# Expert results scaled by their gates and added in DRAM by the scatter itself, with the last norm in the experts' Block

## What is computed

```python
h2 = rmsnorm_2(x, norm2_w)
p_group = softmax(h2 @ wg + bg);  pg, g_sel = top_k(p_group, 1)
top_v, top_i = top_k(expert logits within group g_sel, 2)
gates = softmax(top_v) * pg                      # two gates per token
for each pair (token, expert):                   # 1024 x 2 = 2048 pairs
    y = (silu(h2 @ w_gate[e]) * (h2 @ w_up[e])) @ w_down[e]
    x[token] += gate * y
out = rmsnorm_2(x, norm_f_w)
```

## Time and profile before

| | |
|---|---|
| median of 3 runs | 3539.9 us (3534.38 to 3540.42) |
| profiled execution | 3536.11 us, of which the span from first to last instruction 3534.4 us |
| mean granted TensorE clock | 0.958 |
| experts, from the first gather's issue to the last scatter's | 2882.5 to 3483.1 us |
| last two Blocks, from the last scatter's issue to the end | 3483.05 to 3534.4 us |

### The profile page before, as it was taken

How to read it: one execution, slowest core, us unless ns; L and a number is a source line. 1 busy time by engine, 2 the same in 40 slices (tenths; PEclk the granted TensorE clock), 3 DMA queues, 4 the chain that set the end, 5 groups by cost and what they waited for, 6 DMA issues and landing times. The chain is left out here.

```text
span 3534.4 us, 38476 instructions
## 1 busy us (share of the span) xinstructions
PE 3233.8 (91%) x14690; PEld 2651.4 (75%) x14690; DVE 1920.6 (54%) x2268; ACT 1309.2 (37%) x1660; POOL 326.7 (9%) x356
## 2 busy tenths in 40 slices
PE   6999999899999999999799999969958849999993
PEld 5888888787878888888687778857647738788882
DVE  4344443434345455445511755439636469889985
ACT  4233222312321111111521233325334338888883
POOL 0000000000000000000010000034123101111100
PEclk9999999999999999999899999979979969999996
DMA  3222222242221111111232233342054149999995
GB/s 103 67 67 66 78 84 85 99 157 79 77 84 36 54 53 36 53 54 42 78 117 59 84 106 122 107 164 108 27 181 147 51 159 387 371 372 379 384 363 210
DMA packets 324127, 472.48 MB, mean 134 GB/s; under 512 B 62864, under 2 KB 227216, under 8 KB 321968
## 3 DMA queue, kind: packets, MB, share of 16 engines
q1 hardware_dynamic: 294528, 384.31, 31.9%
q0 software_dynamic: 29488, 86.67, 6.6%
HBM read 414.14 MB, written 73.53 MB: 138 GB/s over the span
## 5 line engine op out<-in xcount | busy, mean ns | idle before, releaser
L1106 DVE TENSOR_TENSOR x_rows<-x_rows,ff_psd 128x512 f32<-128x512 f32 x336 | 228.7, 687 | 304.0 <-PE ff_psd L378 303.9
L376 PE MATMUL m_ps<-h_hl,m_w_hl 128*128 128x512 f32 x896 | 356.4, 398 | 6.7 <-PEq L315 6.7
L377 PE MATMUL m_ps<-h_hl,m_w_hl 128*128 128x512 f32 x896 | 349.9, 391 | 0.0
L378 PE MATMUL m_ps<-h_hl,m_w_hl 128*128 128x512 f32 x896 | 349.9, 390 | 0.0
L2770 DVE TENSOR_TENSOR h_hl<-ex_stage,h_hl 128x1024 fp32r<-128x1024 f32 x256 | 307.3, 1221 | 45.4 <-ACT h_hl L2766 43.9
L2766 ACT ACTIVATE h_hl<-ex_stage 128x1024 fp32r<-128x1024 f32 x256 | 270.7, 1060 | 85.0 <-DMA ex_stage<-in_exp_w_up_dram 39.4
L376 PE MATMUL n_turned<-h_hl,pc_w_hl 128*128 128x512 f32 x576 | 225.8, 392 | 6.6 <-DVE pc_w_hl L1479 6.6
L377 PE MATMUL n_turned<-h_hl,pc_w_hl 128*128 128x512 f32 x576 | 224.9, 390 | 0.0
L378 PE MATMUL n_turned<-h_hl,pc_w_hl 128*128 128x512 f32 x576 | 224.7, 390 | 0.0
L376 PEld LDWEIGHTS m_ps<-h_hl,m_w_hl 128*128 128x128 f32 x896 | 168.9, 189 | 45.5 <-DVE m_w_hl L353 7.1
L1081 ACT ACTIVATE ff_act_hl<-ff_act 128x1024 fp32r<-128x1024 f32 x22 | 23.3, 1060 | 473.9 <-DVE ff_act L1130 473.9
(11 more groups left out here) (524 smaller groups left out, 7562.9 us busy)
## 6 DMA issues: line engine op xcount, KB each, us to landing
ex_stage<-in_exp_w_gate_dram SPq DMA_DIRECT2D x128, 512.0 KB, 5.7
ex_stage<-in_exp_w_up_dram SPq DMA_DIRECT2D x128, 512.0 KB, 6.5
ex_stage<-in_exp_w_down_dram SPq DMA_DIRECT2D x128, 512.0 KB, 6.3
m_stage<-in_w_in_dram SPq DMA_DIRECT2D x56, 512.0 KB, 4.5
pc_stage<-in_w_in_dram SPq DMA_DIRECT2D x36, 512.0 KB, 3.8
ff_stage<-in_w_ffn_down_dram SPq DMA_DIRECT2D x22, 512.0 KB, 3.6
ff_stage<-in_w_ffn_gate_dram SPq DMA_DIRECT2D x21, 512.0 KB, 4.7
ff_stage<-in_w_ffn_up_dram SPq DMA_DIRECT2D x21, 512.0 KB, 5.9
```

What stands on the lines that cost most here:

```text
L376: nc.tensor.matmul(out, w_hl[0], x_hl[0], start=first, stop=False)
L377: nc.tensor.matmul(out, w_hl[0], x_hl[1], start=False, stop=False)
L378: return nc.tensor.matmul(out, w_hl[1], x_hl[0], start=False, stop=last)
L1106: v.tensor_tensor(dst, dst, ps_d[g % NB][:], ALU.add).then_inc(s_add, 1)
```

## The change

The gate moves from the last stage into the experts, the sum of the two experts' rows moves from DVE into the scatter, and the two last Blocks go.

- `mlstm_chunks` also stores each finished tile of x to a DRAM tensor `scr.sum` (`sums_out`, on SP).
- Gates by place: POOL writes `in_tile` anew, now with the gate in place of the pair's number (`place_gates`, 16 instructions), PE forms the 16 products with `in_slot` after expert 0's gate product, ACT copies the result to `scr.place_gate`. `in_slot` lies in `ys`, not in `xg`, so it survives until then, and the gather of expert 1 no longer waits for the routing's end.
- `rows_out` multiplies by the place's gate while it copies.
- `store` scatters by token row (`scr.lst`) into `scr.sum` with `compute_op=ALU.add`: the DMA adds to what stands there. An expert holds a token at most once, and each scatter waits until the one before it has landed.
- Further tiles run in the experts' Block, with the experts' buffers, behind a branch on each engine.
- The last norm runs there too: SP waits for all scatters, loads 8 tiles of the sum into `x_tm`, ACT and DVE norm them, SP stores them from `x_tm`. The gain is loaded, and the table of Sqrt (`warm`), before that.

The program of the further tiles, here left out, is that of before with other buffers and the scatter as above.

```diff
@@ mlstm_chunks, SP
+            def sums_out(t):
+                sp.wait_ge(d_add, 2 * t + 2)
+                sp.dma_start(scr.sum[t * P:(t + 1) * P, :], x_tm[:, t]).then_inc(s_sum, 16)
+
             for k in range(2, NC):
                 chunk_loads(k)
+                if k >= 4:
+                    sums_out(k - 4)
+            for t in range(NC - 4, NC):
+                sums_out(t)
+            sp.wait_ge(s_sum, 16 * NC)
@@ route
-    in_slot = mem.xg[:].rearrange("p b (j n) -> p (b j) n", n=P)
+    in_slot = mem.ys[:].rearrange("p b (j n) -> p (b j) n", n=P)
+    def place_gates(pool):
+        pool.wait_ge(mem.s_gates, 1)
+        for j in range(2 * T):
+            t, n = divmod(j, 2)
+            nc.gpsimd.tensor_scalar(in_tile[:, t, n], io[:, 0:NT], tl[:, n, t:t + 1], scr.gate[:, n, t:t + 1], ALU.is_equal,
+                                    ALU.mult).then_inc(mem.s_placed, 1)
-            ch.inc(v.tensor_copy(scr.row[:], pair))
@@ experts, SP, behind the loads of the weights
+            sp.dma_start(rowg[:], A.norm_f_w_2.rearrange("(a n) -> a n", a=1).broadcast_to([P, D])).then_inc(s_g, 16)
+            for b in range(2):
+                sp.wait_ge(s_st[b], 16 * (NE // 2))
+            sp.wait_ge(s_all, 1)
+            for t in range(T):
+                sp.dma_start(x_tm[:, t], scr.sum[t * P:(t + 1) * P, :]).then_inc(s_y[t], 16)
+            for t in range(T):
+                sp.wait_ge(s_res, t + 1)
+                sp.dma_start(out[t * P:(t + 1) * P, :], x_tm[:, t]).then_inc(s_out, 16)
+            sp.wait_ge(s_out, 16 * T)
@@ experts, POOL
             def store(e):
                 pool.wait_ge(s_ys, e + 1)
-                pool.indirect_dma_start(out=scr.ys, out_offset=bass.IndirectOffsetOnAxis(ap=scr.row[:, e:e + 1], axis=0),
-                                        in_=ys[:, e % 2], in_offset=None, bounds_check=PAIRS - 1,
+                if e:
+                    pool.wait_ge(s_st[1 - e % 2], 16 * ((e + 1) // 2))
+                pool.indirect_dma_start(out=scr.sum, out_offset=bass.IndirectOffsetOnAxis(ap=scr.lst[:, e:e + 1], axis=0),
+                                        in_=ys[:, e % 2], in_offset=None, bounds_check=ROWS - 1, compute_op=ALU.add,
                                         oob_is_err=False).then_inc(s_st[e % 2], 16)
+            nc.gpsimd.memset(xg[:], 0.0).then_inc(s_zero, 1)
+            nc.gpsimd.memset(eps[:], EPS).then_inc(s_eps, 1)
...
-                if e == 0:
-                    pool.wait_ge(mem.s_routed, 1)
+                if e == 1:
+                    mem.place_gates(pool)
...
-            for b in range(2):
-                pool.wait_ge(s_st[b], 16 * (NE // 2))
+            pool.wait_ge(mem.s_routed, 1)
+            n = pool.value_load(count, min_val=0, max_val=NX)
+            with pool.If(n > 0):
...
+            pool.sem_inc(s_all, 1)
@@ experts, ACT
                         x_high(e + 1, 1 - b)
+                        if first:
+                            act.wait_ge(s_pm, 1)
+                            nc.scalar.activation(scr.place_gate[:], mem.ps_places, ACT.Copy).then_inc(s_pg, 1)
...
-                nc.scalar.activation(ys[:, b], ps_d[:], ACT.Copy).then_inc(s_ys, 1)
+                act.wait_ge(s_pg, 1)
+                gate = scr.place_gate[:, e:e + 1] if isinstance(e, int) else scr.place_gate[:, bass.ds(e, 1)]
+                nc.scalar.activation(ys[:, b], ps_d[:], ACT.Copy, scale=gate).then_inc(s_ys, 1)
...
+            for_tiles(act, further_start, further)
+            act.wait_ge(s_eps, 1)
+            nc.scalar.activation(warm[:], eps[:], ACT.Sqrt)
+            for t in range(T):
+                act.wait_ge(s_y[t], 16)
+                nc.scalar.activation(square, x_tm[:, t], ACT.Square, accum_out=ssq[:, 0, t:t + 1]).then_inc(s_sq, 1)
+                act.wait_ge(s_sq, t + 1)
+                nc.scalar.activation(ssq[:, 1, t:t + 1], ssq[:, 0, t:t + 1], ACT.Sqrt, scale=1.0 / D, bias=eps[:]).then_inc(s_std, 1)
@@ experts, DVE
+            for_tiles(dve, lambda: dve.sem_inc(x_lo, 1), further)
+            dve.wait_ge(s_g, 16)
+            for t in range(T):
+                dve.wait_ge(s_std, t + 1)
+                v.reciprocal(ssq[:, 2, t:t + 1], ssq[:, 1, t:t + 1]).then_inc(s_rs, 1)
+                dve.wait_ge(s_rs, t + 1)
+                v.scalar_tensor_tensor(x_tm[:, t], x_tm[:, t], ssq[:, 2, t:t + 1], rowg[:], ALU.mult, ALU.mult).then_inc(s_res, 1)
@@ experts, PE
+            def place_gates():
+                for j in range(2 * T):
+                    pe.wait_ge(mem.s_placed, j + 1)
+                    last = nc.tensor.matmul(mem.ps_places, mem.in_slot[:, j], mem.in_tile[:, j // 2, j % 2], start=j == 0,
+                                            stop=j == 2 * T - 1)
+                last.then_inc(s_pm, 1)
...
                     hidden(e, b, ps_g, 0)
+                    if isinstance(e, int) and e == 0:
+                        place_gates()
                     if not (last and b == 1):
                         turn(e + 1, 1 - b)
@@ program
-        routed_experts(nc, A, scr, hl)
-        further_tiles(nc, A, scr)
-        combine(nc, A, scr, x_tm, out[0])
+        routed_experts(nc, A, scr, hl, x_tm, out[0])
```

More of the change, by code:

```diff
@@ L2719, in expert_memory, with experts @@
     return mem
-def experts(nc, A, scr, c, block, mem):
+def experts(nc, A, scr, c, block, mem, x_tm, out):
     NE, D, F = A.exp_w_gate_2.shape[1:]
     KT, FT, NU, NS = D // P, F // P, 12, 6
-    PAIRS = 2 * scr.T * P
+    ROWS, T, NX = scr.T * P, scr.T, scr.NX
     assert NE % 2 == 0 and F == 512 and D == 1024
@@ L2737, in experts, with for_tiles @@
     s_silu, s_act, s_at, s_ah, s_al = (c.sem(f"ex_{n}") for n in ("silu_ready", "act_ready", "act_turned", "act_high", "act_low"))
-    s_ys = c.sem("ex_ys_ready")
+    s_ys, s_zero = c.sem("ex_ys_ready"), c.sem("ex_rows_zeroed")
+    s_pm, s_pg = c.sem("ex_gates_product"), c.sem("ex_gates_by_place")
+    x_w, x_hi, x_lo, x_use = c.sem("fx_w_loaded"), c.sem("fx_w_high"), c.sem("fx_w_low"), c.sem("fx_w_used")
+    x_row, x_xt, x_xh, x_xl = c.sem("fx_row_gathered"), c.sem("fx_rows_turned"), c.sem("fx_x_high"), c.sem("fx_x_low")
+    x_silu, x_act, x_at, x_ah, x_al = (c.sem(f"fx_{n}") for n in ("silu_ready", "act_ready", "act_turned", "act_high", "act_low"))
+    x_ys, x_st, s_all = c.sem("fx_ys_ready"), c.sem("fx_ys_stored"), c.sem("fx_all_stored")
+    rowg, square = c.sb("cb_gain", [P, D]), xg[:, 0]
+    ssq, eps, warm = c.sb("cb_ssq", [P, 3, T]), c.sb("cb_eps", [P, 1]), c.sb("cb_warm", [P, 1])
+    s_y = c.sems("cb_sum_loaded", T)
+    s_g, s_eps, s_sq, s_std, s_rs, s_res, s_out = (c.sem(f"cb_{n}") for n in (
+        "gain_loaded", "eps_ready", "squared", "std_ready", "rstd_ready", "result", "stored"))
+    count = scr.more[0:1, NX:NX + 1]
+    def for_tiles(eng, start, body):
+        eng.wait_ge(mem.s_routed, 1)
+        n = eng.value_load(count, min_val=0, max_val=NX)
+        with eng.If(n > 0):
+            start()
+            with eng.Fori(0, n) as j:
+                body(j)
     def number(e, u):
@@ L2913, in act_low, with further, low @@
                 v.tensor_tensor(a_hl[:, 1], ps_a[:], f32(a_hl[:, 0]), ALU.subtract).then_inc(s_al, 1)
+            def further(j):
+                def low(r):
+                    dve.wait_ge(x_hi, 3 * j + r + 1)
+                    for u in range(4):
+                        last = v.tensor_tensor(w_hl[u][:, 1], stage[:, u], f32(w_hl[u][:, 0]), ALU.subtract)
+                    last.then_inc(x_lo, 1)
+                low(0)
+                dve.wait_ge(x_xh, j + 1)
+                v.tensor_tensor(xs_hl[0][:, 1], ps_x[:], f32(xs_hl[0][:, 0]), ALU.subtract).then_inc(x_xl, 1)
+                low(1)
+                dve.wait_ge(x_silu, j + 1)
+                dve.wait_ge(x_use, 3 * j + 3)
+                v.tensor_tensor(act_f[:], silu[:], ps_u[:], ALU.mult).then_inc(x_act, 1)
+                low(2)
+                dve.wait_ge(x_ah, j + 1)
+                v.tensor_tensor(a_hl[:, 1], ps_a[:], f32(a_hl[:, 0]), ALU.subtract).then_inc(x_al, 1)
             steps(dve, NE // 2, step, end=NE // 2 - 1)
@@ L2976, in _ @@
             down(NE - 1)
+            for_tiles(pe, lambda: pe.sem_inc(x_use, 1), further)
     return ahead, main
[L2981 to L3108 removed]
@@ L3181, in routed_experts @@
-def routed_experts(nc, A, scr, hl):
+def routed_experts(nc, A, scr, hl, x_tm, out):
     with ExitStack() as ctx:
@@ L3187, in routed_experts @@
         chosen = route(nc, A, hl, scr, c, block, mem)
-        ahead, main = experts(nc, A, scr, c, block, mem)
+        ahead, main = experts(nc, A, scr, c, block, mem, x_tm, out)
         ahead()
```

260 lines of the change are left out of this document (80 added, 180 removed).

## The result

| | device us, median (lowest to highest, runs) | ratio to before, 95% interval |
|---|---|---|
| before | 3534.5 (3532.2 to 3541.7, 8) | |
| after | 3552.1 (3547.0 to 3559.8, 8) | 1.0044 [1.0032, 1.0057] |

The changed kernel is slower by 16 to 18 us; 3538 us and "no change" were forecast. The profiled execution is the slowest of its eight, 3559.8 us around a span of 3558.1. Both parts of the change did something large: the tail became 21 us shorter, and the experts' part became some 40 us longer.

The account below looks back on a forecast made before the run. It took PE and the DMA engines both to be full in the experts. Terms -22.7 + 18 + 3 + 1 + 0.5 = -0.2 us gave 3535.9 or 3539.7, forecast 3538 us; own range 3531 to 3546, with rivals 3517 to 3563.

Parts of the forecast that it names:

- +18 us: Experts' scatters: adding charged as one more gather, 19.5 us less 1.5 us taken by free DMA time; between 0 and +43.
- PE's clock unchanged: Experts: a sign of the forecast being right, that PE's clock stays as before; no term in the sum.
- The end, -22.7: After the last scatter: Blocks, loads and gated additions removed, end at 3511.7, so -22.7 us; -19 with a late landing.
- Gates by place, +3: Before the first expert's `turn(1)`: 16 small products on PE, 4.2 us, delay `turn_act(0)`; +3 us, 0 to 6.6.
- POOL against DVE, +1: First expert's start: POOL's operand work stretches DVE's low parts; +1 us, between 0 and 4.6.
- The scale on `ex_ys`, free: Experts: the gate's scale rides on an ACT copy of 1.01 us, with ACT 83% busy; no cost.
- `sums_out` at +0.5: mLSTM stage: storing 8 x 0.5 MB of x, hidden by PE at a DMA share of 0.27; +0.5 us.
- C: Experts' scatters: an adding row costs much more than two passes, extra from 25 us; 3556 us or 3563, chance 0.25.
- B: Experts' scatters: the adding is hidden or cheap, so -18 us in all, 3520 us; chance 0.26.
- D: The end: the merged Block waits as long as before, 5.7 us from landing to first load; 3544 us, chance 0.07.
- periods of about 18.6: Experts: a sign of the forecast being right, about 18.6 us between POOL's gathers.
- a DMA share of 0.99: Experts: a sign of the forecast being right, the DMA engines' busy share at 0.99.

Follow-up runs that it names:

- e1: Changed kernel with the experts' scatters overwriting the token's row instead of adding to it: 3511.0 us, ratio 0.9935.
- e5: Changed kernel with each expert's ranks placed on partitions that spread its rows evenly over the DMA engines: 3519.5 us, ratio 0.9960.
- e2: Changed kernel with rank r at partition 32*(r%4) + r//4 instead of partition r: 3563.8 us, ratio 1.0089.
- e10: Changed kernel with an expert's rows filling DMA engines one after another, 8 rows each, order 0, 8, 2, 10, 4, 12, 6, 14, then odd: 3565.8 us.
- e11: Changed kernel with an expert's rows filling DMA engines one after another, 8 rows each, in the order 0 to 15: 3564.2 us, ratio 1.0077.
- e7: e5 without compute_op=add, so its scatters overwrite instead of adding: 3505.1 us, ratio 0.9913.
- e9: e5 without the gates by place (POOL instructions, PE products and ACT copy left out, results scattered unscaled): 3519.0 us, ratio 0.9952.
- e4: Changed kernel with rank 64h+8c+4l+a at partition 32a+4c+2h+l instead of rank r at partition r: 3527.8 us, ratio 0.9986.
- e8: Changed kernel with its own places, but the two halves of the partitions exchanged for every odd expert: 3546.3 us, ratio 1.0025.

## Why the prediction was wrong

**The step that failed** is "I charge one gather more, 8.39 MB at 403 GB/s = 20.8 us, 0.65 us per expert", which became the term "+18 us". It measured +41 (e1 against after). The price of a row in it held roughly: one pass more, 328 against 159 ns most often, and 23.7 us of mean queue time against the 19.5 charged. What failed is the division by the rate of all sixteen engines, which takes the rows as spread evenly. A mean expert has 64 rows, and its fullest engine has not 64/16 = 4 but 7.4 of them. That the rows' place is the cause is shown by e5 (33 us back with nothing but other places) and by e2, e10 and e11 (12 to 14 us more). With even places adding costs 14 us (e5 against e7), not far from the +18 that the term allowed.

Why a full engine stops the kernel can be reckoned for one expert. PE waits for weights, not for rows (the waits above). The 12 weight units are 12 x 128 = 1536 packets of 4 KB, 96 for each engine. If a unit has landed only when the last engine has done its share, the fullest engine sets the period. An estimate for an engine with 8 rows of the expert: 96 x 0.159 = 15.3 us, and 8 x (0.159 + 0.328) = 3.9 us for gather and scatter, 19.2 us in all; with plain scatters it is 17.8 us, and with 4 adding rows 17.2, less than the 17.7 us of PE's own work. The periods were 19.1 to 19.5 in the changed kernel, 17.8 to 18.0 before. That it is the weight units which the full engines hold up is inferred from this sum and from the placements; the trace doesn't name a packet's engine.

236 rows by (0.328 - 0.159) us = 39.9 us is what the prediction's working gives with the fullest engine in place of the mean, and 41 were measured. That this is so near is in part luck: the product counts the two last experts too, takes no free time off, prices a row at 328 ns where the mean was 365, and has nothing for the clock; for e5 the same product gives 24 us where 14 were measured.

**Left out of the sum: PE's clock.** The prediction had "PE's clock unchanged" and no term for it. Of the 38.1 us between the thirty periods of e1 and of the changed kernel (572.96 - 534.82), PE is busy 532.5 - 522.7 = 9.8 us longer. It spends 20.5 us of its thirty periods at 1.2 GHz, and 6.8 us in e1, which accounts for 6.8 of the 9.8. So a sixth of what the adding costs comes by way of the clock, after the waits.

The other terms:

*The end, -22.7.* It measured -20.9 in the profile. From the first load on, 3558.1 - 3533.9 = 24.2 us passed where the working had 24.4. The rest is the landing, 6.2 us instead of 4.1. The first load was queued within 0.1 us of the landing, as forecast.

*Gates by place, +3.* On PE:

```profile
2900.16 3.67 PE L3103 MATMUL ex_ps_a<-rt_room,ex_ys 128*128 128x48 f32 x32
2903.66 1.06 PE L3066 MATMUL ex_ps_x<-ex_ident,ex_rows 128*128 128x128 f32 x8
...
2913.26 0.66 PE L3097 MATMUL ex_ps_a<-ex_ident,ex_act 128*128 128x128 f32 x4 [3.07 <-DVE ex_act L3024]
```

3.5 us for the products instead of 4.2, and `turn_act(0)` 2.5 us later than in the earlier trace rows; in the kernel's time it is not seen (e9). The POOL operands were badly sized, 4.8 us in all forecast from the earlier trace rows and 13.1 measured. Thirteen of the sixteen took 0.52 to 0.55 us, the three others 3.63, 1.34 and 1.51 (the second row gives the shortest, the median and the longest):

```profile
2885.38 13.06 POOL L2553 TENSOR_SCALAR rt_room<-rt_iota,rt_room,pair_gates 128x48 f32<-128x48 f32 x16
```

```profile
L2553 POOL TENSOR_SCALAR rt_room<-rt_iota,rt_room,pair_gates x16: 517/518/3630, 2885.4 to 2897.9; 128x48 f32<-128x48 f32 x16
```

They ended at 2898.4, only 1.7 us before PE asked.

*POOL against DVE, +1.* DVE lost nothing: under these same POOL instructions its four low parts took 4.64 us together, one started every 1.14 us, and `x_low` took 1.21. It was POOL that lost, though PE did not feel it. Its instruction of 3.63 us began at 2886.45, 0.1 us after DVE's first low part, and ended 0.2 us after the third was done; the other two also began while a low part was running (at 2889.77 and at 2896.32), and none of the thirteen short ones did. In the row that the prediction read, it had been DVE's instruction that was stretched.

```profile
2886.37 4.64 DVE L2809 TENSOR_TENSOR h_hl<-ex_stage,h_hl 128x1024 fp32r<-128x1024 f32 x4
2890.93 1.21 DVE L3001 TENSOR_TENSOR ex_x_hl<-ex_ps_x,ex_x_hl 128x1024 fp32r<-128x1024 f32 x1
```

*The scale on `ex_ys`, free.* It lengthened the copy from 1.01 to 1.10 us and was free in time as far as e1 can show:

```profile
L2949 ACT ACTIVATE ex_ys<-ex_ps_d,place_gates x32: 1093/1100/1119, 2932.8 to 3525.8; 128x1024 f32<-128x1024 f32 x32
```

*All but the adding* came to -23.0 us (e1) where the terms made -18.2; the sign and most of the size were right, and the difference of 5 us is not accounted for by a run (the interval of e1 alone is some 5 us to either side). `sums_out` at +0.5 wasn't tried by itself.

**The rivals.** C's time, 3556, was near the measured 3552, and its sign, periods of 19 and more, was the one that came. Its condition was nearly met too: it wanted an extra of 25 us, a row at 2.3 plain ones, and a row costs 2.06 most often and 2.3 in the mean. But the reason was another: with such rows laid evenly the adding cost 14 us and the periods were 18.0 (e5). B (3520) is nearly the time of e5, 3519.5, though the adding is not hidden even there. D was not seen: the first load followed the landing at once. No rival was an uneven load.

**What would show it.** Forecast: periods of about 18.6, measured 19.5; 25 us of waiting at `turn_act`, measured 38 in 22 experts; a DMA share of 0.99, measured 0.97, and this one I read as a mere check when it was the thing that tells the two mechanisms apart; PE's clock unchanged, measured 0.99 for 1.00 over the 27 periods, worth 7 us; the tail 28 to 30 us, measured 30.4.

**Two readings of the trace before.** The first window of the earlier trace rows holds 26 periods, not 27 (469.1 / 18.04). And the 9.1 us of waits in the earlier trace rows are not the stalls of the 27 periods: they include the 3.9 us at 2910.72, in the first expert. Within the 27 periods PE idled 5.0 us, so the agreement of the two 9.1s was chance; the forecast sum does not use it.

## What to carry to other kernels

A DMA of one row per partition loads its engines as its rows fall on them, and here the transfers that were split over all engines, the weights, came late by the fullest. So cost it as rows on the fullest engine times the packet's time, not as bytes over the core's rate, and add what that engine has to carry besides; for lists shorter than the tile, lay the ranks out so that they go round the engines (here worth 33 us with an adding scatter, 8.5 us without). A DMA share that falls while the waits on DMA grow was here the sign of unevenly loaded engines: look at one transfer's packets before reckoning with totals. Waits of PE can be paid twice, once as idle time and once as stretches at the lower clock, so compare its busy time for the same matmuls too. And an adding scatter costs a little over twice a plain one in DMA time, so it is worth its while where the pass that it saves is on the path and the engines have room.

## What the runs showed of the hardware that I had not expected

- The rows of an indirect DMA belong to engines by partition, and rows that are skipped leave their engine all but empty (a packet of 8 bytes and 8 ns each): 63 rows on 8 engines by 8 (changed kernel), on 16 by 4 (e4).
- Lateness of an engine in one expert is hardly made good in the next, though weights are loaded half an expert ahead (e8, 6 to 9 us of the 33 to 37).
- With idle queues the first adding packets of a scatter take far longer than the later ones, 0.48 to 1.50 us in the changed kernel's last scatter against 0.328, while in e1 the first plain ones took 0.16. The scatter's landing came to 6.2 us after its issue, and in e5, with half as many rows on an engine, to 4.8 at the most (issue at 3487.28, first load at 3492.08).
- Issuing an adding scatter keeps POOL 1.58 us, a plain one 1.01 (1.005 in e1).
- A POOL comparison and product with two scalars per partition on 128x48 mostly took 0.52 us, where DVE's of the same shape in the routing took 0.30. Those that began while DVE was making a low part (128x1024) took 1.3 to 3.7 us, in all nine runs that have them, while the low parts kept their 1.2 to 1.3 us.
- After waits of 1.7 to 2.4 us PE was granted 1.2 GHz for 3.4 us at a time, five times in the experts of the changed kernel and not once between 2935 and 3470 in the kernel before.
